# Moving five steps of a one-core transformer kernel some tiles later

## The reference, cut to what matters

```
first block, each layer:  x += 0.5*swiglu(rmsnorm(x));  x += hybrid_mixer(rmsnorm(x));  x += 0.5*swiglu(rmsnorm(x))
hybrid_mixer(h): u, va, q, k, v, qi, ki, wi, g_a, g_b = split(h @ w_in)
    y_a = (gelu(u) * (tril(w_s) @ layernorm(gelu(va)) + b_s)) @ w_pa          # token mixing
    y_b = attention(rope(q), rope(k), v, top 64 keys by index scores) @ w_pb
    out = (sigmoid(g_a + b)*y_a + sigmoid(g_b + b)*y_b) @ w_out
second block, each layer: h = rmsnorm(x);  c = split(h @ w_in)
    a: softmax attention with summed dilated windows          # the "first unit"
    b: latent attention: q = rmsnorm(cq) @ w_uq, k, v = rmsnorm(ckv) @ w_ukv, 32 rotated channels
    c: compressed, selected and windowed attention, gated
    d: stick breaking: after = reversed running sum of log(1-beta); a = exp(log_sigmoid(z) + after); y = a @ v
    x += sum_i( sigmoid(h @ w_merge_i + b_i) * ((y_i * silu(gate_i)) @ w_branch_i) ) @ w_out
```

## Time and profile before

| | |
|---|---|
| median of three runs | 1665.68 us |
| profiled execution, its own time | 1664.85 us |
| its span in the trace | 1663.1 us |
| TensorE busy | 1599.2 us, 96% |
| GpSimd busy | 1000.4 us, 60% |
| VectorE busy | 503.8 us, 30% |
| ScalarE busy | 366.0 us, 22% |
| transfers' mean share | 50.2% |

### The profile page before, as it was taken

One profiled execution on the slowest core, in us unless ns is written; L12 is line 12 of the kernel. 1 busy time (PEld: TensorE's weight loads), 2 busy tenths in 40 slices (PEclk: granted clock), 3 DMA queues, 4 the chain that ended last, 5 costly groups with the idle time before them and its releaser, 6 DMA issues.

```text
span 1663.1 us, 32224 instructions
## 1 busy us (share of the span) xinstructions
PE 1599.2 (96%) x14172; PEld 1398.7 (84%) x14172; DVE 503.8 (30%) x1128; ACT 366.0 (22%) x902; POOL 1000.4 (60%) x542
## 2 busy tenths in 40 slices
PE   6999999999999999999999999979999999999998
PEld 5888788888888888878888788868887887788887
DVE  3111264343110211126434311133432223533223
ACT  2111124212110211112421211023333122324112
POOL 6777556566777577765556677744264674346571
PEclk9999999999999999999999999979999999999999
DMA  8555444454555465544445455534343554444451
GB/s 354 201 203 203 140 178 156 175 203 160 200 202 201 183 215 199 199 154 162 168 153 202 165 199 199 202 108 157 133 174 127 203 178 166 136 147 169 160 203 51
DMA packets 42619, 294.90 MB, mean 177 GB/s; under 512 B 4720, under 2 KB 6256, under 8 KB 7792
## 3 DMA queue, kind: packets, MB, share of 16 engines
q1 hardware_dynamic: 42480, 292.84, 50.2%
HBM read 291.78 MB, written 1.05 MB: 176 GB/s over the span
## 4 chain that ended last, share of the span: by engine, by line
PE 93%; DVE 4%; ACT 2%; issue 1%; DMA 0%; SPq 0%; DVEq 0%; ACTq 0%
PE ps L510 27%; PE ps L511 26%; PE ps L512 26%; PE ps L528 1%; PE ps L530 1%; PE ps L529 1%; PE ps L596 1%; PE ps L759 1%; PE ps L614 1%; PE ps L602 1%; PE ps L588 1%; PE ps L586 0%; DVE diag L1497 0%; PE ps L549 0%; PE ps L603 0%
## 5 line engine op out<-in xcount | busy, mean ns | idle before, releaser
L486 POOL TENSOR_TENSOR w_low<-ring 128x1024 f16<-128x1024 f32 (+2 forms) x538 | 1000.2, 1882 | 630.3 <-DMA ring<-in_w 630.2
L510 PE MATMUL ps<-hP,ring 128*128 128x256 f16 (+1 forms) x2976 | 822.4, 276 | 11.8 <-DVE hP L1209 11.7
L511 PE MATMUL ps<-hP,ring 128*128 128x256 f16 (+1 forms) x2976 | 821.7, 276 | 0.0
L512 PE MATMUL ps<-hP,w_low 128*128 128x256 f16 (+1 forms) x2976 | 821.4, 276 | 0.0
L510 PEld LDWEIGHTS ps<-hP,ring 128*128 128x128 bf16 (+1 forms) x2976 | 295.6, 99 | 59.4 <-DVE hP L1209 13.7
L511 PEld LDWEIGHTS ps<-hP,ring 128*128 128x128 bf16 (+1 forms) x2976 | 295.4, 99 | 37.9
L512 PEld LDWEIGHTS ps<-hP,w_low 128*128 128x128 f16 (+1 forms) x2976 | 295.4, 99 | 37.3
L511 PE MATMUL ps<-work,ring 128*128 128x256 f16 x1088 | 296.7, 273 | 0.0
L510 PE MATMUL ps<-work,ring 128*128 128x256 f16 x1088 | 296.5, 272 | 0.0
L512 PE MATMUL ps<-work,w_low 128*128 128x256 f16 x1088 | 296.3, 272 | 0.0
L1242 DVE TENSOR_TENSOR ps<-work,ps 128x256 f32<-128x256 f32 x88 | 37.8, 429 | 342.9 <-PE ps L512 312.0
(11 more groups left out here) (199 smaller groups left out, 1142.8 us busy)
## 6 DMA issues: line engine op xcount, KB each, us to landing
ring<-in_w SPq DMA_DIRECT2D x268, 1024.0 KB, 4.8
con<-in_const SPq DMA_DIRECT2D x1, 2732.0 KB, 16.5
gm<-in_gm SPq DMA_DIRECT2D x2, 1024.0 KB, 16.9
ring<-in_w SPq DMA_DIRECT2D x2, 640.0 KB, 5.7
ring<-in_w SPq DMA_DIRECT2D x2, 560.0 KB, 3.7
ring<-in_w SPq DMA_DIRECT2D x2, 544.0 KB, 3.7
xT<-in_x SPq DMA_DIRECT2D x4, 256.0 KB, 4.0
out<-work SPq DMA_DIRECT2D x8, 128.0 KB, 2.0
```

The source lines that it names most:

```text
L486: nc.gpsimd.tensor_tensor(w_low[:, c % SLOTS, a:b], ring[:, c % SLOTS, a:b], w_high[:, c % SLOTS, a:b], ALU.subtract).then_inc(split.by((c ...
L510: nc.tensor.matmul(bank, w_high[:, slot, a:a + m], rhs(k, 0), start=(k == 0), stop=False)
L511: nc.tensor.matmul(bank, w_high[:, slot, a:a + m], rhs(k, 1), start=False, stop=False)
L512: mm = nc.tensor.matmul(bank, w_low[:, slot, a:a + m], rhs(k, 0), start=False, stop=(k == kt - 1))
```

## The change

The first order list moves `qc` 0 ahead of `rkv`. In the A stages two more `gb` tiles stand ahead of the token mixing. In the B stages the first unit's turn moves behind `bk` and `bv`, and its `mix` behind `bq` 0, `bq` 1 and `kc` 0; one more merge tile stands ahead of the running sums, and the merge tiles behind them move along. ScalarE's and VectorE's lists are rewritten to match. At the start the halving of the biases moves behind the sums of squares. No instruction is added or taken away.

```diff
@@ TILES_B
-           ("ag", 0), ("ag", 1), ("rkv", 0), ("qc", 0), ("qc", 1), ...
+           ("ag", 0), ("ag", 1), ("qc", 0), ("rkv", 0), ("qc", 1), ...
@@ TensorE, mixer_a
                     gemm("gb", 0), gemm("gb", 1), gemm("gb", 2)
+                    gemm("gb", 3), gemm("gb", 4)
                     pe.wait_ge(*y_low.at((s, 1)))
...
-                    for n in range(3, 8):
+                    for n in range(5, 8):
                         gemm("gb", n)
@@ TensorE, mixer_b
-                    gemm("lat", 0), gemm("ag", 0), gemm("ag", 1), gemm("rkv", 0), gemm("qc", 0), gemm("qc", 1)
-                    turn(s, "a")
+                    gemm("lat", 0), gemm("ag", 0), gemm("ag", 1), gemm("qc", 0), gemm("rkv", 0), gemm("qc", 1)
                     for n in range(4):
                         gemm("bk", n)
                     gemm("bv", 0), gemm("bv", 1)
+                    turn(s, "a")
+                    gemm("bq", 0), gemm("bq", 1), gemm("kc", 0)
                     mix(s, "a", lambda t, h: a_v[:, t, h * HD:h * HD + HD])
-                    gemm("bq", 0), gemm("bq", 1), gemm("kc", 0)
                     turn_pairs("bq", 0)
...
-                    merge(0, 3), merge(0, 4), merge(0, 5)
+                    merge(0, 3), merge(0, 4), merge(0, 5), merge(0, 6)
                     pe.wait_ge(*stick_sp.at(s))
...
-                    merge(0, 6), merge(0, 7)
+                    merge(0, 7), merge(1, 0)
                     pe.wait_ge(*stick_probs.at(s))
@@ ScalarE, mixer_a
-                    take("gb", 0), take("gb", 1), take("gb", 2)
+                    for n in range(5):
+                        take("gb", n)
...
@@ ScalarE, mixer_b
-                    take("rkv", 0), take("qc", 0), take("qc", 1)
+                    take("qc", 0), take("rkv", 0), take("qc", 1)
+                    take("bv", 0), take("bv", 1)
                     copy_turned(s, "a")
-                    take("bv", 0), take("bv", 1)
-                    y_parts(0)
                     copy_raw("bq", 0), copy_raw("bq", 1)
                     take("kc", 0)
+                    y_parts(0)
...
-                    merge(0, 4), merge(0, 5), merge(0, 6)
+                    merge(0, 4), merge(0, 5), merge(0, 6), merge(0, 7)
                     act.wait_ge(*stick_exponent.at(s))
                     nc.scalar.activation(probsT, ps[:, 4:8, 0:PACK], ACT.Exp).then_inc(stick_probs.by(s), 1)
-                    merge(0, 7)
-                    merge(1, 0)
+                    merge(1, 0), merge(1, 1)
                     y_parts(3)
@@ VectorE, mixer_b
                     dve.wait_ge(*mixed.at((s, "a")))
+                    ra(0)
                     gated_y(0)
-                    ra(0)
+                    ra(1)
                     y_parts(0)
-                    ra(1)
                     rb(0)
...
-                    merge(0, 5)
+                    merge(0, 5), merge(0, 6)
                     dve.wait_ge(*stick_sums.at(s))
...
-                    merge(0, 6), merge(0, 7)
+                    merge(0, 7), merge(1, 0)
                     dve.wait_ge(*stick_mixed.at(s))
@@ VectorE, start
+                for n in range(1, DK - 1):
+                    add_square("F0", n)
                 dve.wait_ge(par_landed, 16)
                 a = PAR["b_gate"][0]
                 nc.vector.tensor_scalar(half_bias[:, :], ...
-                for n in range(1, DK - 1):
-                    add_square("F0", n)
```

More of the change, by code:

```diff
@@ L882, in mixer_b @@
                     mm.then_inc(stick_sums.by(s), 1)
-                    merge(0, 6), merge(0, 7)
+                    merge(0, 7), merge(1, 0)
                     pe.wait_ge(*stick_probs.at(s))
                     mix_values(lambda t, h: d_v[:, t, h * HD:h * HD + HD]).then_inc(stick_mixed.by(s), 1)
-                    for br in range(1, 4):
-                        for n in range(DK):
-                            merge(br, n)
+                    for p in range(9, 32):
+                        merge(p // DK, p % DK)
                     pe.wait_ge(*merged.at((s, 2, DK - 1)))
@@ L1157, in mixer_b @@
                     nc.scalar.activation(ps[:, 4:8, 0:PACK], ps[:, 4:8, 0:PACK], ACT.Ln, bias=1.0).then_inc(stick_ln.by(s), 1)
-                    merge(0, 4), merge(0, 5), merge(0, 6)
+                    merge(0, 4), merge(0, 5), merge(0, 6), merge(0, 7)
                     act.wait_ge(*stick_exponent.at(s))
                     nc.scalar.activation(probsT, ps[:, 4:8, 0:PACK], ACT.Exp).then_inc(stick_probs.by(s), 1)
-                    merge(0, 7)
-                    merge(1, 0)
+                    merge(1, 0), merge(1, 1)
                     y_parts(3)
-                    for p in range(9, 24):
+                    for p in range(10, 24):
                         merge(p // DK, p % DK)
@@ L1589, in mixer_b @@
                     y_parts(3)
-                    for p in range(8, 24):
+                    for p in range(9, 24):
                         merge(p // DK, p % DK)
```

## The result

The changed kernel took 1651.79 us (median of six runs, 1650.62 to 1652.70). Before it stood at 1662.95 in the same comparison (six runs, 1658.88 to 1666.33): the ratio is 0.9914, with an interval of 0.9897 to 0.9932, so 0.9% faster. The forecast was 1652.7 with a range of 1649.0 to 1659.5. The profiled execution took 1651.31 us (span 1649.5), 13.54 less than the profiled execution before, where the sum had said 12.15.

The account below looks back on a forecast made before the run. TensorE, busy 96% of the span, was taken to bound the kernel. Terms -4.6 - 1.65 - 4.3 - 3.0 - 0.5 + 2.4 - 0.5 = -12.15 took 1664.85 to 1652.7 us, range 1649.0 to 1659.5.

Parts of the forecast that it names:

- the clock away from the four waits: Stretches other than those behind TensorE's two mixing and two sums waits: no clock change was counted there, 0 us.
- Token mixing: A stages: two more gb tiles remove waits of 2.2 and 2.4 us, saving 4.6, plus 1.65 of clock in A1.
- Running sums: B stages: waits of 2.9 us become 0.75 on ScalarE's tanh, saving 4.3, plus 3.0 of clock in B0.
- The latent's spread: B stages: qc 0 covers waits of 0.35 us in B1 and 0.15 in B0, saving 0.5.
- First unit: B stages: moved mix makes TensorE wait 0.6 us before the first rotation and 0.7 before bq 3; loss 1.2 each, 2.4.
- Start: Kernel start: first TensorE instruction near 8.2 us, not 11.0, then a wait for GpSimd; gain 0.5, bounds 0.3 to 2.0.
- Clock behind the four waits and the first unit: Full clock expected behind mixing, sums and B stages' first unit; 1.65 us saved in A1 and 3.0 in B0.
- the clock's share isn't won: Thin matmuls of mixing and sums, not idle time, lower the clock; only waits are saved: 1657.3 us, chance 0.13.
- The measure: The sum was made against one profiled execution of the kernel before, 1664.85 us, 0.8 below the median of three runs.
- The slower rival: Sparse stretches lower the clock wherever they are, at mixing, sums and both first units: +3.15 us, 1668.0, chance 0.05.

Follow-up runs that it names:

- the three kernels of its set: Changed kernel with first unit's turn and mix put back (1646.28 us); with only VectorE's list reordered (1647.06); with turn and mix back and one tanh moved earlier (1645.65).

## Where the prediction was right, and where it failed

**The step that failed is the clock away from the four waits.** The sum took the 4.65 us behind two of the waits (1.65 in A1, 3.0 in B0) for the whole of what the clock would do, and put every other stretch at nothing without giving a reason, though the clock also falls at the norms and at the hidden products in the trace of before (0.92 over that stretch). The runs showed that the clock's share of those stretches changed by as much as that behind the waits. By the first TensorE instruction of each norm, in the two profiled executions:

| stages | forecast | measured |
|---|---|---|
| to A0's first instruction | -0.5 | -0.68 (192.19 to 191.51) |
| A0 | -2.2 | -2.27 (182.06 to 179.79) |
| A1 | -2.4 - 1.65 | -4.32 (183.82 to 179.50) |
| F1, F2, F3 | 0 | -0.58 - 0.26 - 1.33 |
| N1 and B0, and B1 | -5.4 | -3.57 (282.89 to 279.32) and -0.67 (270.31 to 269.64) |
| N2 | 0 | +0.15 |

No edit touches F1 to F3, and there 2.2 us came that nobody had forecast: the clock was low for 3.4 us in place of 6.8 at the norms of F1 and F3. In the B stages 2 x 1.63 us were lost in the hidden products' stretch, which no edit touches either. On the way from the norm to that stretch some 1.5 came back: it took 100.5 us in B0 and 90.9 in B1 before, and 100.6 and 90.9 after, in spite of new waits of 1.0 in each, less the 0.5 of the spread in both; the low stretch behind the norm began 1.3 to 1.4 us sooner in the stage. These unforecast terms nearly cancel, so that the total came out within 1.4 us of the forecast between profiled executions, and within 1.0 between medians, is in part luck. What was right is the terms that were worked out from the waits:

- **Token mixing: right, its cause incomplete.** Both waits went, and the clock behind A1's. The prediction took VectorE's two slow products as given. They are what makes the wait, and they are not in every stage of every run.
- **Running sums: right.** The new wait is 0.70 where 0.75 was computed, and the sums started straight behind the tile. B0's clock share of 2.98 came: 10.17 us after 13.24.
- **The latent's spread: right**, 0.5 with the gap too small for the table.
- **First unit: right in place and sign, priced a little too high.** Expected were 0.6 ahead of the rotation and 0.7 ahead of `bq` 3. In B0 of the changed kernel:

```profile
1157.38 0.42 DVE L1264 TENSOR_TENSOR work<-ps,con 96x256 f32<-96x256 f32 x1 [8.35 <-PE ps L603]
...
1157.95 0.64 PE L614 MATMUL ps<-work,con 96*96 96x256 f32 x2 [0.60 <-DVE work L1264]
...
1160.61 0.67 PE L753 MATMUL ps<-work,ring 128*96 128x256 f32 x2 [0.38 <-DVE work L1428]
```

  VectorE had stood idle for 8.35 us when the mix came, with the cosines of `bq` 0 free to do: that is the loss. The second wait was 0.38 because TensorE came to it at 2.9 us behind the mix and not at 2.65. Waits of 1.0 in each layer, not 1.2.
- **Start: right in its waits, its gain of 0.5 not shown.** First instruction at 8.1 (forecast 8.2), a gap of 1.0 for GpSimd. The 0.68 us of the table is one pair of executions: A0's norm began at 191.4 to 192.2 us in the four traces with the old start and at 190.9 to 193.0 in the eight with the new one. It goes with the moment at which TensorE comes to its full pitch (0.11 us between matmuls): at 20.2 to 22.1 us in the four, at 20.4 to 23.7 in the eight. The prediction named this moment, with bounds for its coming sooner only.
- **Clock behind the four waits and the first unit: right.** It was low at none of them. The rival "the clock's share isn't won" fails there, by the 9 of 15 and 0 of 33.
- **The measure.** The profiled execution before was 1.9 us above the median of its six runs, and the one after 0.5 below, so 13.5 between profiled executions became 11.2 between medians. A forecast from one execution of a kernel that spreads by 7 to 15 us carries this.

The slower rival had its mechanism in part: thin matmuls do bring the clock down, at the hidden products, which it didn't name and where they did so before the change too; at the mixing, the sums and the first unit they did not.

## What stays open

Why the stretch of the hidden products is low for 3.4 us longer in some executions wasn't settled. The changed kernel's twelve runs all lie within 2.1 us although its two profiled executions differ in it (in the second, B0 had 40.49 us and F3's stage was 1.8 us longer). The low stretches ahead of N2 add to the same 71.7 us in both, and to 64.9 in those of the three kernels of its set. So in the changed kernel the amount of low clock repeats and its place doesn't; why is open. One thing goes with the length of the low stretch at the hidden products: where the clock fell 3.6 to 4.6 us after their first matmul it stayed down for 10.2 us (6 cases), where it fell after 4.9 to 5.8 us, for 6.8 (14 cases). What sets that moment, these runs don't show. A comparison of profiled executions can tell the place of it, not the cause.

## What to carry to other kernels

Where one engine bounds the kernel, its table of waits prices the waits of an edit to a few tenths of a microsecond, new ones included (0.70 for 0.75, 0.60 for 0.6, 0.38 for 0.7), if each engine's list is walked through from the moment the moved work is free. It doesn't price the clock elsewhere in the kernel, which here lost 3.3 us in one place and gave back some 3.7 in others; a forecast needs a range for that. A wait moved past on the bounding engine must be moved past on the helper too: here VectorE stood 8.35 us ahead of a wait with free work behind it, and putting that work first took both new waits away. An idle time of over 2 us of TensorE can cost as much again through the clock (1.5 to 3.0 us, in 9 of 15 cases), so cover these first.

## What the runs showed of the hardware

- Idle of 2.2 to 2.9 us, with thin matmuls behind it, was followed by a granted clock of 0.50 (1.2 GHz) in 9 of 15 cases, at a cost of 1.5 to 3.0 us each; the same matmuls with idle time of 0.7 us or none never were (0 of 33).
- 32 float32 matmuls of 15 columns (64 records, 8.4 to 10.4 us), with no idle time, had the clock fall within them in every trace, and so did two groups of 16 with a full tile between them.
- VectorE's 128x512 product of two SBUF inputs took 0.69 us with GpSimd idle and 2.27 beside its splitting, on the same line in the same stage.
- Over the runs of the kernel before, the granted clock and the time go together: 0.969 with 1670.2 to 1672.7 us, 0.976 with 1656.3 to 1659.1.
